# Weight slabs of all units as high and low parts, with GpSimd making some of the low ones

## The reference

```
h = rmsnorm(x, norm_g) * (1 + scale) + shift          # shift, scale, gate: silu(cond) @ w_ada + b_ada
z = h @ w_in                                          # 1024 -> 6912 columns, split into the parts below
A: y = a * sigmoid(g); depthwise conv (31 taps); layernorm; silu;  br_a = (y * silu(conv_gate)) @ w_conv_out
B: S5 state space, 32 groups, two directions, 64 complex states; gelu; GLU (w_ssm_glu);
                                                      br_b = (y * silu(ssm_gate)) @ w_ssm_out
C: attention, 8 query and 2 key heads of 64, rmsnorm of q and k, rotary for the latent stream,
   the latent stream also reads 128 cached keys;      br_c = (o * silu(attn_gate)) @ w_attn_out
mixed = sum over the branches of sigmoid(merge) * br
x = x + gate * (mixed @ w_out)
```

## Time and profile before

| | us |
|---|---|
| median of three runs | 714.88 |
| the profiled execution | 713.04 |
| its span | 711.0 |
| TensorE busy | 652.4 |
| VectorE busy | 551.5 |
| ScalarE busy | 297.3 |
| GpSimd busy | 36.4 |
| mean granted TensorE clock | 0.969 of full |

### The profile page before, as it was taken

How to read it: one execution, slowest core, us unless ns; L and a number is a source line. 1 busy time by engine, 2 the same in 40 slices (tenths; PEclk the granted TensorE clock), 3 DMA queues, 4 the chain that set the end, 5 groups by cost and what they waited for, 6 DMA issues and landing times. The chain is left out here.

```text
span 711.0 us, 9584 instructions
## 1 busy us (share of the span) xinstructions
PE 652.4 (92%) x3573; PEld 466.5 (66%) x3573; DVE 551.5 (78%) x1024; ACT 297.3 (42%) x454; POOL 36.4 (5%) x49
## 2 busy tenths in 40 slices
PE   3689899996997999998999899999897999999997
PEld 1368674553843688877887687465664578877885
DVE  3679689989777886589975657998878698887663
ACT  2564350212533445435455736011445444436441
POOL 2100001111000000010001010012000000010000
PEclk9989889998998999999999999999998999999999
DMA  8992817654383274654543437660632346655631
GB/s 289 348 275 70 275 36 232 239 183 141 123 272 122 75 229 146 179 176 149 167 158 95 138 136 252 205 240 11 198 112 66 89 121 184 199 165 164 201 104 59
DMA packets 67305, 117.65 MB, mean 165 GB/s; under 512 B 11052, under 2 KB 15484, under 8 KB 67260
## 3 DMA queue, kind: packets, MB, share of 16 engines
q1 hardware_dynamic: 66980, 116.94, 51.9%
q10 hardware_dynamic: 280, 0.11, 0.1%
HBM read 112.51 MB, written 1.38 MB: 160 GB/s over the span
## 5 line engine op out<-in xcount | busy, mean ns | idle before, releaser
L805 PE MATMUL proj<-raw,hT 128*128 128x512 f32 (+1 forms) x320 | 132.0, 558 | 0.0
L1584 DVE SCALAR_TENSOR_TENSOR cvacc<-cvpad,taps,cvacc 128x256 f32<-128x256 f32 x240 | 98.6, 477 | 0.3
L805 PEld LDWEIGHTS proj<-raw,hT 128*128 128x128 f32 x320 | 58.2, 190 | 58.8 <-issue 57.0
L1477 DVE TENSOR_TENSOR raw_split<-raw,wide_split 128x1024 fp32r<-128x1024 f32 x56 | 67.9, 1220 | 21.6 <-ACT wide_split L1193 20.9
L1193 ACT ACTIVATE wide_split<-raw 128x1024 fp32r<-128x1024 f32 x56 | 58.6, 1059 | 55.9 <-PE proj L835 55.9
L834 PE MATMUL proj<-raw_split,H_split 128*128 128x512 f32 x192 | 75.4, 393 | 0.0
L833 PE MATMUL proj<-wide_split,H_split 128*128 128x512 f32 x144 | 57.9, 402 | 4.7 <-DVE raw_split L1477 4.7
L835 PE MATMUL proj<-wide_split,H_split 128*128 128x512 f32 x144 | 56.9, 395 | 0.0
L1477 DVE TENSOR_TENSOR raw_split<-raw,utok_split 128x1024 fp32r<-128x1024 f32 x28 | 34.2, 1220 | 15.1 <-ACT utok_split L1193 15.1
L1193 ACT ACTIVATE utok_split<-raw 128x1024 fp32r<-128x1024 f32 x28 | 29.6, 1058 | 34.8 <-PE proj L835 34.8
L834 PEld LDWEIGHTS proj<-raw_split,H_split 128*128 128x128 f32 x192 | 36.4, 190 | 7.3
(11 more groups left out here) (252 smaller groups left out, 1327.0 us busy)
## 6 DMA issues: line engine op xcount, KB each, us to landing
raw<-in_w_in SPq DMA_DIRECT2D x104, 512.0 KB, 4.3
raw<-in_w_ada SPq DMA_DIRECT2D x48, 512.0 KB, 5.3
raw<-in_w_out SPq DMA_DIRECT2D x16, 512.0 KB, 3.8
raw<-in_w_ssm_glu SPq DMA_DIRECT2D x8, 512.0 KB, 7.0
raw<-in_w_ssm_out SPq DMA_DIRECT2D x8, 512.0 KB, 4.3
raw<-in_w_attn_out SPq DMA_DIRECT2D x8, 512.0 KB, 3.7
raw<-in_w_conv_out SPq DMA_DIRECT2D x8, 512.0 KB, 3.7
raw<-in_w_in SPq DMA_DIRECT2D x8, 256.0 KB, 3.7
```

The source lines that it names most:

```text
L805: m = T.matmul(proj.bank((l, u, s))[:, 0:n], lhs[:, s, kt, :], w[:, i, :], start=(kt == 0), stop=last)
L1477: return V.tensor_tensor(out, a, b, op)
L1584: m = V.scalar_tensor_tensor(acc, src, taps[:, t, j:j + 1], acc, ALU.mult, ALU.add)
```

## The change

All units become split units. The plain path goes. `low_on_pool` gives the low parts of q, kv, sg, ag ("zone"), gg, glub, glua ("att") and of the merges B0, B1, C0 (both me and br) to GpSimd; the others stay with VectorE. Each kind has a list of rooms, now in gates, H and pre too. The tokens exist only as hTh and hTl (new tiles); hT is a transient in mixed. geT is written in two parts. tA and tB lie in HY, the loads of b in pre.

Moved besides: the bbar products from VectorE to GpSimd, ahead of UT (in layer 1 they stay ahead of ca); the sums of squares of q and k from VectorE to ScalarE (`sumsq`, ten Square activations per stream with accumulation, before K 0 and before K 1); the norm and rotary of k from VectorE to GpSimd (`k_norm`, semaphore k_done); q's factor from the rows into the exp's scale. The first two HY copies (stage HY) now come directly after the scan, ahead of unit ag's evacuation, of qkn and of the taps. Conv taps: 4 and 0 in the zone (were 16 and 8), 10 in Y (18), 28 and 20 in att 0 and att 1 of layer 0 (40 and 22), 20 and 20 in layer 1 (30 and 22), the rest, 62 and 74, in the merges (28 and 46). In layer 0 the taps stage moves behind preE, the first cg piece ahead of hT.

```diff
+ZONE = ("q", "kv", "sg", "ag")
+IN_ATT_UNITS = ("gg", "glub", "glua")
+ROOM_KINDS = {"early": ("g0", "g2", "h2", "g1", "h3"), "zone": ("g1", "p0", "p1"), "att": ("h0", "h1", "h2", "h3"),
+              "late": ("wa", "wb", "ut"), "wout": ("wa", "wb", "ut", "cv")}
-TAPS_IN_ZONE = (16, 8)
-TAPS_IN_ATT = (((8, 8, 8, 8, 8), (7, 4, 4, 7, 0)), ((6, 6, 6, 6, 6), (7, 4, 4, 7, 0)))
+TAPS_IN_ZONE = (4, 0)
+TAPS_IN_Y = (0, 4, 6)
+TAPS_IN_ATT = (((8, 8, 5, 5, 2), (5, 5, 5, 5, 0)), ((6, 6, 3, 3, 2), (5, 5, 5, 5, 0)))
...
+            + [("UT",), ("S",), ("cp",), ("bz", 0), ("convT", 0), ("convT", 1), ("unit", "q"), ("unit", "kv"), ("adaE", l, 2),
+               ("sumsq", 0), ("K", 0), ("bz", 1), ("unit", "sg"), ("sumsq", 1), ("K", 1), ("scan", 0, NCHUNK), ("HY",),
+               ("unit", "ag")] + nxt("adaE", n, 0)
+            + [("qkn",), ("conv", TAPS_IN_ZONE[l]), ("Y",), ("adaT", l, 2)] + nxt("adaT", n, 0)
...
+def low_on_pool(u):
+
+    return u in ZONE or u in IN_ATT_UNITS or u[2:] in ("B0", "B1", "C0")
...
+            def slab_work(key):
+                if key[0] == "ada":
+                    ada_slab(key)
+                    return
+                l, u, kp = key
+                if kp == 0:
+                    for s in range(NS):
+                        proj.claim(pe, (l, u, s))
+                for kt in range(KT_SLAB * kp, KT_SLAB * kp + KT_SLAB):
+                    split_products(l, u, kt, geTs if u[:2] == "gl" else hTe, range(NS))
...
+                elif k == "sumsq":
+                    s = stg[1]
+                    proj.drained(act, (l, "q", s))
+                    proj.drained(act, (l, "kv", s))
+                    for i in range(HEADS + KV):
+                        h = i // 2 + 4 * (i % 2) if i < HEADS else i
+                        m = S.activation(sq_out[:, s, HD * i:HD * i + HD], qk[:, s, HD * i:HD * i + HD], ACT.Square,
+                                         accum_out=qst[:, s, 0, h:h + 1])
+                    m.then_inc(qk_sq, 1)
...
                     if stg == LAST_COMB:
+                        if l + 1 < DEPTH:
+                            act.wait_ge(pre_done, 2 * (l + 2))
                         merged_high(l, 0)
...
+            def low_parts(upto):
+
+                for m in range(lows[0], upto):
+                    if low_on_pool(pieces[m][1]):
+                        pool.wait_ge(piece_hi, m + 1)
+                        tt_(piece_slot(m, raws), piece_raw(m), piece_high(m).bitcast(F32),
+                            ALU.subtract).then_inc(piece_lo[1], 1)
+                    lows[0] = m + 1
...
+                elif k == "UT":
+                    low_parts(piece_at[(l, "q", 1)])
+                elif k == "unit" and stg[1] in ZONE:
+                    low_parts(ahead(l, stg[1]))
+                elif k == "HY":
+                    low_parts(ahead(l, "ag"))
+                elif k == "att":
+                    low_parts(ahead(l, "glua" if stg[1] else "gg"))
+                elif k == "comb":
+                    low_parts(ahead(l, "br" + stg[1] + str(stg[2]), 0))
+                elif k == "bbar":
+                    pool.wait_ge(pre_done, 2 * (l + 1))
+                    pool.wait_ge(tab_done, 1)
...
+                    tt_(t0, b0, co[1])
+                    link(tt_(t1, b1, co[1]))
+                    tt_(b0, b0, co[0])
+                    link(tt_(b1, b1, co[0]))
+                    tt_(b0, b0, t1, ALU.subtract)
+                    tt_(b1, b1, t0, ALU.add).then_inc(bbar_done, 1)
```

More of the change, by code:

```diff
@@ L65, in order @@
     begin = [("unit", "cg"), ("tabB",), ("tabC",), ("bT", 0), ("cT", 0), ("unit", "ssm"), ("pre", 0, 0),
-             ("chunks", "ca", 4), ("pre", 0, 1), ("unit", "ca"), ("taps", 0), ("preE", 0, 0), ("pack",), ("preE", 0, 1)]
+             ("chunks", "ca", 4), ("pre", 0, 1), ("unit", "ca"), ("preE", 0, 0), ("pack",), ("preE", 0, 1), ("taps", 0),
+             ("bbar", 0)]
     if l:
@@ L152, in units_of, with kind_of @@
     return []
-def split_unit(u):
-    return u[:2] in ("me", "br", "wo") or u in EARLY
+def kind_of(u):
+    if u in EARLY:
+        return "early"
+    if u in ZONE:
+        return "zone"
+    if u in IN_ATT_UNITS:
+        return "att"
+    return "wout" if u[:2] == "wo" else "late"
+def low_on_pool(u):
+    return u in ZONE or u in IN_ATT_UNITS or u[2:] in ("B0", "B1", "C0")
 def side_uses(l, stage):
@@ L419, in build @@
         slab_used = sem("slab_used")
-        pieces = [key for key in order_of_slabs if key[0] != "ada" and split_unit(key[1])]
+        pieces = [key for key in order_of_slabs if key[0] != "ada"]
         piece_at = {key: m for m, key in enumerate(pieces)}
         piece_hi = sem("piece_hi")
-        piece_lo = sem("piece_lo")
+        piece_lo = [sem("piece_lo_dve"), sem("piece_lo_pool")]
         piece_used = sem("piece_used")
@@ L580, in build @@
         for l, stg in todo:
-            if stg[0] in ("split", "brT"):
+            if stg[0] == "geT":
+                parts += [(l, "geT", s) for s in range(NS)]
+            elif stg[0] == "brT":
                 parts.append((l,) + stg)
@@ L1102, in _ @@
                     for u, nk, n in units_of(stg):
-                        if not split_unit(u):
+                        if k == "unit" and u not in EARLY:
                             for key in slab_keys(l, stg):
@@ L1563, in qk_norm @@
-                dve.wait_ge(qk_done, ls(l, s))
+                    return
+                link(m)
+                dve.wait_ge(rope_in, 16)
+                tt_(qkt[:, 0:W].rearrange("p (h d) -> p h d", d=HD), q3, rope[:, 0:1, :].to_broadcast([P, HEADS, HD]))
+                for a in range(2):
+                    five = lambda t: t.rearrange("p (h f a c) -> p a h f c", f=2, a=2, c=16)
+                    sin = rope[:, 1, :].rearrange("p (o f a c) -> p a o f c", o=1, f=2, a=2)[:, a]
+                    m = tt_(five(q_turn)[:, a], five(qk[:, s, 0:W])[:, 1 - a], sin.to_broadcast([P, HEADS, 2, 16]))
@@ L1565, in gelu_sum @@
+                link(m)
+                tt_(qk[:, s, 0:W], qkt[:, 0:W], q_turn, ALU.add).then_inc(qk_done, 1)
             def gelu_sum(l, s):
@@ L1883, in _ @@
                                           side.bank(key)[:, 0:2 * nk * P]).then_inc(side.freed(key), 1)
[L1884 to L1890 removed]
+                        if s == 0 and p in (2, 3):
+                            gelu_sum(l, p - 2)
                         if s == 1 and p == 4:
```

344 lines of the change are left out of this document (164 added, 180 removed).

## The result

The change makes the kernel slower: 770.77 us median of 4 runs (770.48 to 772.02) against 714.34 us, the median of 4 runs of the kernel before (709.03 to 714.9), a ratio of 1.081 with a 95% interval of 1.076 to 1.087. The profiled execution took 771.05 us, its span is 769.2, against 713.04 and 711.0.

What follows compares the result with a forecast made beforehand. TensorE bounds merges; in the zones TensorE and VectorE run as two chains of nearly equal length. Zones -11 and -1, attention -10, merges +2 sum to -20: median 714.88 becomes 694.5 us, range 664 to 742.

Steps and rivals of the forecast that it cites:

- The price that decides: GpSimd beside VectorE: Wherever GpSimd subtracts beside VectorE: each subtraction costs VectorE 1.05 us, from possible values of nothing to 2.0.
- The pivot: Price per GpSimd subtraction, 1.4 us, at which the predicted sum is zero and from which the full collision decides.
- The second rival, collision in full: Scan and taps: GpSimd holds VectorE off for its whole 2.0 to 2.3 us; slower, 753 or middle 738; chance 0.31.
- case without collision: Whole kernel: subtractions cost VectorE nothing and TensorE sets both zones; -34 us, 681, or 672; chance 0.22.
- the zones: Each layer from the transposes after the state products to the first Y product: -11 us in layer 0, -1 in layer 1.
- just inside windows: Attention: VectorE's 23 us in either half of layer 0 fits; -5 us per layer of TensorE's 6.2, -10 in all.
- TensorE saves 34 us at most: Split instead of plain products in q, sg, ag, kv and attention: 17 us per layer, an upper bound for the gain.
- Y near 164: End of layer 0's zone: Y starts at 163.8 us instead of 174.93, a gain of 11 us.
- Sums of squares that make TensorE wait 2.4 us twice: Zone: 20 small ScalarE activations per layer stand ahead of the K copies; TensorE waits some 2.4 us twice for side banks.
- the power row: Trace before: two VectorE products kept 1.02 us under GpSimd's 2.39 us power, read as reading costing, not length.
- the first rival: No collision: subtractions cost VectorE nothing, the scan keeps 36 us; 681, or 672; chance 0.22.
- GpSimd as the bound (709): Merges: at 3.1 us per piece instead of 2.72, TensorE loses 14 us on 36 pieces; 709; chance 0.09.

Runs made afterwards that it cites:

- run 1: The changed kernel without GpSimd's 84 subtractions, TensorE multiplying by the high part in the low part's place: 699.75 us, ratio to before 0.981.
- experiment 12: The changed kernel without its GpSimd subtractions, but with a power of ten elements per partition in each one's place, which nobody waits for: 700.44 us.
- before_both: Kernel before, with the first two HY copies ahead of the norms, taps ahead of Y unchanged, half of M's transfers issued by GpSimd: 707.30 us, ratio 0.989.

## Why the prediction was wrong

**The step that failed is "The price that decides: GpSimd beside VectorE".** It took 1.05 us of VectorE per subtraction, "between the first two, which are nearest to the row", from copies that read one operand, and scaled them by elements. Measured: 1.55 as the mean over the changed kernel ((624.8 - 495.0) / 84), and where VectorE had instructions with two SBUF operands to do all the time, which is where the prediction's sums apply the price, 2.2 (CP and scan) and 2.1 (taps). The pivot stood at 1.4. The nearest row was a row of another kind: the copies of this case cost VectorE 0.39 of their length, subtractions 0.61 on average, and in a full stretch nearly all. The second rival, collision in full, had the mechanism, the place (scan and taps) and the sign, with a chance of 0.31.

**The price explains most of the miss.** At 2.0 us the prediction's own sum is 753, already above its range; the rival's middle of 738 was too low because it stood for a lower price. Against its own case without collision (681) the sum at 2.0 charges 72 us for the subtractions, and the runs show 71.0. That the total agrees so well is in part luck: it charges the zones 34, attention 16 and the merges 23, where leaving the subtractions out gave 20.4, some 18 and 32.7. What is left:
- The base was too low. Without any collision the prediction had 681 or 672; run 1 shows 699.75, 19 us more, about what is missing from 753 to 770.77. Of this, 7.8 us were the 20 transfers of M, the last of which SP issues at 166.94 and which no step named: TensorE's own end, forecast for 161.5, was 165.1, Y began at 168.78. 4.9 us were ScalarE's high part of q's first slab ahead of the packing, an instruction that the change adds to a queue and that the prediction costed as "nothing" for ScalarE but for the sums of squares. Some 6 us of it stay unexplained.
- Attention was costed by totals: "just inside windows". The forecast put it 2 us above its case without collision; the runs give some 18. The tiny nmx product on its critical path went from 169 ns [the kernel before] to 738.
- In the merges VectorE's share alone was summed. GpSimd is kept out by a run of taps as well (6.46 us for a subtraction), TensorE waits, and VectorE idles 12.82 us later: the two losses follow each other instead of overlapping.
- The clock was no term of the prediction. TensorE is busy for 639.0 us with the same 3765 records that take 626.5 without subtractions, at a mean granted clock of 0.927 against 0.969. What part of the 71.0 us that is, no run separates.

**Point by point.** TensorE saves 34 us at most: not tested as such; with nothing colliding and both queues mended the kernel is 27.7 us under before (684.93 against 712.62 beside it), so the bound held. A subtraction of 2.3 us: 2.40 undisturbed, right. Scan steps of 1.3 to 1.5 us instead of 1.06: on average (175.67 - 124.80) / 32 = 1.59. Y near 164 in layer 0: 177.89; near 506 in layer 1: 546.39. The products of kv pace with their columns, 0.12 us each: right. Sums of squares that make TensorE wait 2.4 us twice: 3.2 and 0.4 in layer 0 of run 1 and 2.3 once in layer 1, so 4.8 per layer was too much. GpSimd busy for 210 to 240 us: 273.4, as its subtractions are held too. Bbar on GpSimd and HY ahead of the norms: right, the latter is the 7 us that can be had. That the reading costs and not the length, from the power row: right, and confirmed by experiment 12. Of the signs, taps that lengthen in groups and TensorE idle before cback (6.5 us, for the conv result of layer 1) came. The scan took 50.9 and 51.2 us, neither the 36 of the first rival nor the 60 of the second: that limit was set too high. And TensorE was idle for VectorE and GpSimd inside the merges too, not only at the end of the zones. GpSimd as the bound (709): no, but as late for TensorE 5 us at most.

## What to carry to other kernels

Before work goes to GpSimd, list what VectorE does at that time. If that has two operands in SBUF, count the whole length of a GpSimd subtraction (2.4 us here) against VectorE, twice what the same subtraction costs on VectorE itself (1.22 us), and look for tiny instructions on a critical path that would wait behind it. Memsets and powers of few elements cost such instructions nothing here, issuing ten transfers per layer neither; copies cost under a third. Taking the work back to VectorE is no cure by itself: it recovered 16 of 71 us. When one chain is shortened, ask which transfer's issue ends just before the old bound: here 20 transfers at 0.64 us stood 2 us behind TensorE, and an edit of the order alone gave 1% where the whole change lost 8%.

## What was not expected of the hardware

- A VectorE copy with one SBUF operand (0.22 to 2.38 us) and a tensor_scalar (434 to 935 ns) are held by a GpSimd subtraction as well, while a reciprocal with one SBUF operand (203 and 203 ns) and a product with one operand in PSUM (687 and 682 ns) are not. The same copy is held by a memset (0.60 us beside one of 0.52), which leaves taps alone.
- The exclusion is mutual and not fair by time: 20 taps back to back keep their 0.40 us and stretch a subtraction to 6.46 us; the 22 of the next merge are held by nine subtractions, 1.28 us each on average.
- 84 GpSimd powers of 2.27 us cost VectorE nothing (busy 491.8 us against 495.0); 84 subtractions of 2.55 us cost it 131 us.
- GpSimd issues its ten transfers of M in 0.5 to 0.74 us each (the groups of before_both), no slower than SP's 0.64.
